# Expert picks in fewer VectorE instructions, two steps per dot, in a one-core decoder layer

## The chip, the cores and the metric

The kernel runs on one core of one Trainium2 chip. The metric is the device time of one execution in microseconds, the median of the runs shown; below it is better.

## What is computed

One layer of a decoder on 256 tokens of width 2048 in float32: a combined projection, three attentions (sliding window with sinks, block-sparse, indexed sparse), gates, an output projection, and then a channel mixer (PEER) with a residual, and a last RMS norm. The change lies in the channel mixer:

```python
def peer_ffn(h, w_q, sub_keys, u_tab, v_tab):
    q = (xt @ w_q).reshape(n, PEER_HEADS, 2, PEER_QDIM // 2)
    s = jnp.einsum("nhpd,hpkd->nhpk", q, sub_keys)           # 8 heads, 2 x 128 scores
    s1, i1 = lax.top_k(s[:, :, 0], PEER_TOPK)                # 16 of 128
    s2, i2 = lax.top_k(s[:, :, 1], PEER_TOPK)
    cand_s = (s1[..., :, None] + s2[..., None, :]).reshape(n, PEER_HEADS, 256)
    cand_i = (i1[..., :, None] * PEER_KEYS + i2[..., None, :]).reshape(n, PEER_HEADS, 256)
    top_s, pos = lax.top_k(cand_s, PEER_TOPK)                # 16 of 256
    experts = jnp.take_along_axis(cand_i, pos, axis=-1)
    g = jax.nn.softmax(top_s, axis=-1)
    a = jax.nn.gelu(jnp.einsum("td,thkd->thk", xc, u_tab[ec]))
    return jnp.einsum("thk,thkd->td", gc * a, v_tab[ec])
```

Each token and head picks 16 of 16384 experts. The expert's row of `u_tab` (2048 floats, 8 KB) is multiplied with the token's hidden vector, the sum goes through a gelu, is weighted with the softmax of the scores, and multiplies the expert's row of `v_tab`.

## The kernel before

The program has one hand-written instruction stream per engine, joined by semaphores. It goes through the weight matrices first: TensorE multiplies, ScalarE and VectorE split every float32 block into a high and a low part (lines 550 and 905). This takes some 740 us. At the end, from about 1590 us on, `v_tab` is streamed as dense blocks and multiplied with a matrix of coefficients (line 1486). Between the two lies the expert stage, which the change touches.

**Units.** The 256 tokens are two tiles of 128 (one token per partition), and there are 8 heads, so 16 units; unit c is tile c // 8 and head c % 8. For a unit, the picks (`pick_step`, lines 1075 to 1131) find the 16 expert numbers, GpSimd gathers 16 times 128 rows of `u_tab` (1 MB each), and VectorE makes 16 dots (`dot`, line 1133), one for each gather: the 2048 products of row and hidden vector, summed per partition, 128 tokens at a time.

**GpSimd.** `phase` (lines 524 to 531) waits until the unit's indices are there (`idx_ok`), copies them to `stage_u` (line 526), and issues the 16 gathers (line 530). The landing place is `u_ring`, four slots of 1 MB. Gather k waits until dot k-4 is done (`dot_ok`), so at most four gathers are ahead of the dots. All instructions are in order: gather 0 of the next unit comes after gather 15 of this one and the copy.

**VectorE.** `phase` (lines 1167 to 1177) runs the 16 dots of unit c, and behind dot k it does step k of the picks of unit c+1. A pick has 13 steps (`PICK_STEPS`): 0 to 3 find 16 of 128 scores in both halves (max, max_index, match_replace) and add all pairs to `cand`; 4 to 7 find 16 of the 256 sums; 8 to 10 turn the positions into two key numbers by comparing with a row of 0 to 15, multiplying with the keys found, and summing, and write `key_all` and `idx_all`; 11 and 12 make the softmax from ScalarE's exponentials. Each step begins with a drain, an instruction that lets VectorE finish what is before it. Step 0 waits for the scores' copy (`sw_ok`). Before dot 0, `gelu_argument` (line 1138) forms the cubic argument of the gelu's tanh for the unit before in three small instructions, ScalarE takes the tanh, and behind dot 0 `coefficients` (line 1147) finishes the unit's coefficients. The first pick (unit 0) runs alone, without dots.

**ScalarE.** At the start of the stage it is in the loop over the 16 blocks of the query projection (lines 783 to 803). It moves TensorE's results out (lines 787 and 789), and between blocks it does the exponentials (`exps_of`), the copy of a unit's scores for the picks (`scores_of`) and the tanh (`tanh_of`) of units 0 to 2. These wait for VectorE, and what is behind them waits too. The scores of unit 1 are copied after block 3; those of unit 2 after block 5, and of unit 3 after block 15, the end of the loop. TensorE's next block needs the evacuation of the block before (`qp_ev`). Afterwards a hardware loop over units follows, and from unit 8 on (`phase`, line 840) ScalarE also builds the one-hot matrices of tile 0 (lines 810 to 823).

**SP.** It issues the loads of the query weights during the first units, and of `v_tab`'s first blocks as the last four dots free the ring (line 446).

Of the kernel before, what the change touches and what calls it, by code (L numbers as in the profile page):

```python
# [30 lines left out]
ALU = mybir.AluOpType  # L31
# [75 lines left out]
def build(nc, x, rel_bias, g_mix, w_in, a_sinks, c_lat_gain, c_w_uk, c_w_uv, w_br_a, w_br_b, w_br_c,  # L107
# [86 lines left out]
    tif = at("tif", 202.3125, [P, 2, PTOP])  # L194
# [3 lines left out]
    thlf = at("thlf", 202.6875, [P, 2, PTOP])  # L198
    esel = at("esel", 202.8125, [P, 2, PTOP])
    eidx = at("eidx", 202.9375, [P, PTOP])  # L200
    texp = at("texp", 203, [P, PTOP])
# [4 lines left out]
    tsum = at("tsum", 203.75, [P, 8])  # L206
# [107 lines left out]
    dot_ok = sem("dot_ok")  # L314
    arg_ok = sem("arg_ok")
# [225 lines left out]
    def _(act):  # L541
# [212 lines left out]
        def exps_of(u):  # L754
            act.wait_ge(top_ok, u + 1)
            nc.scalar.activation(texp[:, :], texp[:, :], ACT.Exp, accum_out=tsum[:, 0:1]).then_inc(ex_ok, 1)
# [26 lines left out]
        for w in range(2 * PH):  # L783
# [67 lines left out]
        phase(PH)
        with act.Fori(PH + 1, NU - 2) as c:
            phase(c)
        phase(NU - 2, scoring=False)
        phase(NU - 1, picking=False, scoring=False)
        tanh_of(NU - 1)
# [26 lines left out]
    def _(dve):  # L883
# [190 lines left out]

        def pick_step(u, step):
# [445 lines left out]
```

## Time and profile before

| | us |
|---|---|
| timed runs | 2371.70, 2367.78, 2370.84 (median 2370.84) |
| span of the profiled execution, first to last instruction | 2368.5 |
| VectorE busy in the span | 1492.5 |
| GpSimd busy | 570.1 |
| one dot, custom instruction of line 1135 (256 of them) | 2.284 |
| first dot, last dot (start) | 783.4, 1588.7 |

The profile records one execution; its own device time is not listed beside the span, and the three timed runs lie between 0.7 us below and 3.2 us above the span. A unit of the expert stage can be followed in a timeline from one dot 0 to the next. Times of instructions on GpSimd count from their start to the end of the work on the engine; for a gather that is when it is issued completely, not when its rows have landed. When rows landed can be read where a dot waited for them: it starts then.

### The profile page before, as it was taken

Reading aid. Unit: us, or ns where it says so; the run is one execution under the profiler, and the core shown is the slowest. Engines: PE = TensorE matmul, PEld = TensorE weight load, DVE = VectorE, ACT = ScalarE, POOL = GpSimd, SP = SyncE. Lnnn points to the kernel's source line nnn. Section 1 sums busy time; section 2 is a strip of 40 time slices with the busy share of each in tenths; the row PEclk is TensorE's granted clock in tenths of the full one; section 3 lists DMA queues with packets and bytes.
Section 4 is the critical chain, followed back from the end, with each engine's and each line's share of the span. In section 5 each row is a group of like instructions: output and inputs, shape, how many; then the busy total and the mean of one; then the engine's idle time right before and its main releaser. Section 6 shows DMA issues by size and latency. Waiting matters only on the chain.

```text
span 2368.5 us, 28340 instructions
## 1 busy us (share of the span) xinstructions
PE 1662.7 (70%) x9817; PEld 1478.0 (62%) x9817; DVE 1492.5 (63%) x2175; ACT 850.4 (36%) x1353; POOL 570.1 (24%) x338
## 2 busy tenths in 40 slices
PE   7999999999998980000011111116999999999997
PEld 6999999999987870000011111115888888888886
DVE  5554444445644788999989999879444444444445
ACT  5444444444343100000044344343334444334443
POOL 0000000001600246676666776640000000000000
PEclk9999999999999995555555555559999999999999
DMA  9555566555576999999989899890555556555553
GB/s 305 152 166 164 168 171 171 169 164 159 179 260 202 370 341 339 340 338 343 331 327 343 328 340 338 318 352 25 173 193 195 195 189 242 191 193 195 195 189 112
DMA packets 300663, 560.38 MB, mean 237 GB/s; under 512 B 9452, under 2 KB 238877, under 8 KB 250430
## 3 DMA queue, kind: packets, MB, share of 16 engines
q1 hardware_dynamic: 260926, 282.20, 37.2%
q0 software_dynamic: 39184, 276.84, 31.4%
q8 instruction: 35, 0.57, 0.1%
q10 hardware_dynamic: 496, 0.58, 0.1%
q14 instruction: 22, 0.18, 0.0%
HBM read 555.34 MB, written 8.44 MB: 238 GB/s over the span
## 4 chain that ended last, share of the span: by engine, by line
PE 60%; DVE 21%; DMA 6%; issue 6%; DVEq 3%; POOL 3%; ACT 1%; POOLq 0%; SPq 0%; ACTq 0%
PE ps L1486 30%; PE ps L1231 20%; DVE u_ring L1135 14%; DMA u_ring<-in_peer_u,stage_u 6%; PE ps L1391 4%; PE ps L1413 3%; DVEq L1081 2%; POOL u_ring L530 1%; DVE ones L1162 1%; POOL stage_u L526 1%; PE ps L1336 1%; PE ps L1317 1%; PE ps L1326 0%; DVE esel L1121 0%; POOL msum L517 0%
## 5 line engine op out<-in xcount | busy, mean ns | idle before, releaser
L1135 DVE CUSTOM_DVE_ANT_0 u_ring<-u_ring,h 128x2048 f32<-128x2048 f32 x256 | 583.9, 2284 | 56.8 <-DMA u_ring<-in_peer_u,stage_u 56.3
L530 POOL DMA_INDIRECT u_ring<-in_peer_u,stage_u x256 | 471.8, 1843 | 306.1 <-DVE dots L1135 247.9
L905 DVE TENSOR_TENSOR w_lo<-raw,w_hi 128x2048 fp32r<-128x2048 f32 x112 | 259.1, 2314 | 332.2 <-ACT w_hi L550 332.0
L1231 PE MATMUL ps<-act_hi,w_hi 128*128 128x256 f32 x1536 | 441.1, 287 | 4.9 <-DVE act_lo L1030 2.9
L1231 PE MATMUL ps<-act_hi,w_lo 128*128 128x256 f32 x1536 | 435.3, 283 | 0.0
L1231 PE MATMUL ps<-act_lo,w_hi 128*128 128x256 f32 x1536 | 435.2, 283 | 0.0
L1486 PE MATMUL ps<-v_hi,c_hi 128*128 128x512 f32 x1024 | 400.4, 391 | 4.1 <-DVE v_lo L1204 4.1
L1486 PE MATMUL ps<-v_lo,c_hi 128*128 128x512 f32 x1024 | 400.7, 391 | 0.0
L1486 PE MATMUL ps<-v_hi,c_lo 128*128 128x512 f32 x1024 | 400.5, 391 | 0.0
L871 ACT ACTIVATE v_hi<-u_ring 128x2048 fp32r<-128x2048 f32 x126 | 241.5, 1917 | 417.1 <-PE ps L1486 417.1
L1462 PE MATMUL ps<-ones 128*128 128x128 f32 x512 | 105.0, 369 | 326.8 <-ACT ones L822 310.2
L550 ACT ACTIVATE w_hi<-raw 128x2048 fp32r<-128x2048 f32 x112 | 214.1, 1912 | 264.2 <-PE ps L1231 219.3
L1462 PEld LDWEIGHTS ps<-ones 128*128 128x128 f32 x512 | 89.7, 264 | 342.4 <-issue 232.5
L1231 PEld LDWEIGHTS ps<-act_hi,w_hi 128*128 128x128 f32 x1536 | 295.2, 192 | 6.1 <-issue 4.0
L1231 PEld LDWEIGHTS ps<-act_lo,w_hi 128*128 128x128 f32 x1536 | 295.4, 192 | 0.3 <-issue 0.2
L1231 PEld LDWEIGHTS ps<-act_hi,w_lo 128*128 128x128 f32 x1536 | 295.1, 192 | 0.0
L1204 DVE TENSOR_TENSOR v_lo<-u_ring,v_hi 128x2048 fp32r<-128x2048 f32 x128 | 292.4, 2285 | 0.0
L1202 DVE TENSOR_TENSOR c_lo<-ct,c_hi 128x256 fp32r<-128x256 f32 x128 | 54.5, 425 | 366.0 <-ACT c_hi L872 366.0
L1454 PE MATMUL ps<-ident,key_all 128*128 128x128 f32 x4 | 1.4, 442 | 321.9 <-DVE cw_all L1153 321.9
L1486 PEld LDWEIGHTS ps<-v_hi,c_hi 128*128 128x128 f32 x1024 | 192.8, 188 | 51.2 <-issue 4.3
L1486 PEld LDWEIGHTS ps<-v_lo,c_hi 128*128 128x128 f32 x1024 | 193.0, 188 | 40.9
L1486 PEld LDWEIGHTS ps<-v_hi,c_lo 128*128 128x128 f32 x1024 | 193.1, 189 | 37.6
(204 smaller groups left out, 1588.5 us busy)
## 6 DMA issues: line engine op xcount, KB each, us to landing
u_ring<-in_peer_v SPq DMA_DIRECT2D x128, 1024.0 KB, 4.9
raw<-in_w_in SPq DMA_DIRECT2D x80, 1024.0 KB
raw<-in_w_out SPq DMA_DIRECT2D x16, 1024.0 KB
wq_raw<-in_peer_w_q SPq DMA_DIRECT2D x16, 1024.0 KB, 8.4
raw<-in_w_br_a SPq DMA_DIRECT2D x16, 512.0 KB
bias_by_query<-bias_by_distance POOLq DMA_DIRECT2D x1, 4096.0 KB, 21.0
bias_st<-bias_by_query POOLq DMA_DIRECT2D x16, 256.0 KB, 4.7
raw<-in_w_br_b SPq DMA_DIRECT2D x16, 256.0 KB
```

The lines of the kernel that those rows point to most:

```text
L530: pool.indirect_dma_start(u_ring[:, k % RING], None, u_tab, bass.IndirectOffsetOnAxis(ap=stage_u[:, par, k:k + 1], axis=0)).then_inc(u_in[ ...
L550: nc.scalar.activation(w_hi[:, j % NHL], raw[:, j % NRAW], ACT.Copy).then_inc(hi_done, 1)
L871: nc.scalar.activation(v_hi[:, j % NHL], u_ring[:, j], ACT.Copy)
L905: nc.vector.tensor_tensor(w_lo[:, j % NHL], raw[:, j % NRAW], w_hi[:, j % NHL].bitcast(F32), ALU.subtract).then_inc(lo_done, 1)
L1135: nc.vector.tensor_tensor_reduce(out=u_ring[:, k % RING], in0=u_ring[:, k % RING], in1=h2[:, tile], scale=1.0, scalar=0.0, op0=ALU.mult, o ...
L1202: nc.vector.tensor_tensor(c_lo[:, j % NHL], ct[:, span(RING * i + j, 1)].rearrange("p a t -> p (a t)"), c_hi[:, j % NHL].bitcast(F32), ALU ...
L1204: nc.vector.tensor_tensor(v_lo[:, j % NHL], u_ring[:, j], v_hi[:, j % NHL].bitcast(F32), ALU.subtract).then_inc(vl_ok, 1)
L1231: last = nc.tensor.matmul(out_ap, w_parts[wp][:, slot, k], act_parts[ap][:, k], start=(k == k0 and m == 0), stop=(k == k1 - 1 and m == 2))
L1391: last = nc.tensor.matmul(ps[:, 2 * (c % 2) + t, :], mg_parts[ap][:, T * k + P * t:T * k + P * t + P], w_wide[wp][:, j % NHL, kk], start=( ...
L1413: last = nc.tensor.matmul(ps[:, J + w % 2, cols], wq_raw[:, (w + NWQ // 2) % NWQ, k], h2T[:, k, cols], start=(k == 0), stop=(k == NK - 1))
L1462: last = nc.tensor.matmul(ps[:, 6 + par, PKEYS * m:PKEYS * m + PKEYS], ones[:, 1, par, m], ones[:, 0, par, m], start=True, stop=True)
L1486: last = nc.tensor.matmul(ps[:, 4 * t + c, :], c_parts[cp][:, j % NHL, P * t:P * t + P], v_parts[vp][:, j % NHL, WIDE * c:WIDE * c + WIDE] ...
```

## The change

Four things are changed, all in the expert stage.

1. The picks use fewer instructions. The indices stay uint32 where they were cast to float32 (`tif`, `thlf`, `eidx` are gone); the two comparisons of 256 elements become one of 512, and the two multiplications likewise; the sum is written to `key_all` directly, and the expert number to `idx_all`. The subtraction of the largest score goes to ScalarE, as the bias of the exponential (`ntop`), which also writes to `cw_all` directly. The scaling by the reciprocal of the sum moves from step 12 into `coefficients`, the half of the gelu into the dot's scale.
2. The gelu's argument: ScalarE squares the dots (`tanh_of`), VectorE needs one instruction after it in place of three. It is done behind dot 0, before it was ahead of it, and the coefficients follow behind dot 1, before behind dot 0.
3. Behind dot k come the steps 2k and 2k+1 of the picks, so they are through behind dot 6. In unit 0 (`first`) they begin behind dot 3.
4. ScalarE's two loops over units are unrolled in Python, since the place of the sum (`tsum`) alternates.

```diff
-        def exps_of(u):
+        def exps_of(u, par):
             act.wait_ge(top_ok, u + 1)
-            nc.scalar.activation(texp[:, :], texp[:, :], ACT.Exp, accum_out=tsum[:, 0:1]).then_inc(ex_ok, 1)
+            nc.scalar.activation(ntop[:, :], ts[:, 0:1], ACT.Copy, scale=-1.0).then_inc(nt_ok, 1)
+            act.wait_ge(nt_ok, u + 1)
+            nc.scalar.activation(cw_all[:, span(PTOP * u, PTOP)], ts[:, :], ACT.Exp, bias=ntop[:, 0:1],
+                                 accum_out=tsum[:, par:par + 1]).then_inc(ex_ok, 1)
...
-        def tanh_of(u):
+        def tanh_of(u, par):
+            act.wait_ge(dot_ok, PTOP * u + PTOP)
+            nc.scalar.activation(gel[:, 0], dots[:, par], ACT.Square, scale=2.0 * math.sqrt(0.044715)).then_inc(sqd_ok, 1)
             act.wait_ge(arg_ok, u + 1)
-            nc.scalar.activation(gel[:, 1], gel[:, 0], ACT.Tanh, scale=math.sqrt(2.0 / math.pi)).then_inc(th_ok, 1)
+            nc.scalar.activation(gel[:, 1], gel[:, 0], ACT.Tanh, scale=2.0 * math.sqrt(2.0 / math.pi)).then_inc(th_ok, 1)
...
-        with act.Fori(3, PH) as c:
-            tanh_of(c - 2)
-            exps_of(c)
+        for c in range(3, PH):
+            tanh_of(c - 2, c % 2)
+            exps_of(c, c % 2)
             scores_of(c + 1)
...
             elif step == 3:
                 for s in range(2):
                     nc.vector.max_index(ti[:, s, 8:16], tv[:, s, 8:16], sc_r[:, s])
+                wait(dve, ex_ok, u)
                 nc.vector.tensor_tensor(cand[:, :, :], tv[:, 0].unsqueeze(2).to_broadcast([P, PTOP, PTOP]),
                                         tv[:, 1].unsqueeze(1).to_broadcast([P, PTOP, PTOP]), ALU.add)
             elif step == 4:
                 nc.vector.max(ts[:, 0:8], flat)
-                nc.vector.tensor_copy(tif[:, :, :], ti[:, :, :])
...
             elif step == 7:
-                nc.vector.max_index(tp[:, 8:16], ts[:, 8:16], flat_r)
-                nc.vector.tensor_scalar(texp[:, :], ts[:, :], ts[:, 0:1], None, ALU.subtract).then_inc(top_ok, 1)
+                nc.vector.max_index(tp[:, 8:16], ts[:, 8:16], flat_r).then_inc(top_ok, 1)
             elif step == 8:
                 nc.vector.tensor_scalar(thl[:, 0], tp[:, :], 4, None, ALU.logical_shift_right)
                 nc.vector.tensor_scalar(thl[:, 1], tp[:, :], PTOP - 1, None, ALU.bitwise_and)
-                dve.drain()
-                nc.vector.tensor_copy(thlf[:, :, :], thl[:, :, :])
             elif step == 9:
-                for s in range(2):
-                    nc.vector.tensor_tensor(pick[:, s], thlf[:, s].unsqueeze(2).to_broadcast([P, PTOP, PTOP]),
-                                            iota_f[:, 0:PTOP].unsqueeze(1).to_broadcast([P, PTOP, PTOP]), ALU.is_equal)
-                dve.drain()
-                for s in range(2):
-                    nc.vector.tensor_tensor(pick[:, s], pick[:, s], tif[:, s].unsqueeze(1).to_broadcast([P, PTOP, PTOP]), ALU.mult)
+                nc.vector.tensor_tensor(pick[:, :, :, :], thl[:, :, :].unsqueeze(3).to_broadcast([P, 2, PTOP, PTOP]), iota_pick,
+                                        ALU.is_equal)
             elif step == 10:
-                nc.vector.tensor_reduce(esel[:, :, :], pick[:, :, :, :], AX.X, ALU.add)
-                dve.drain()
-                nc.vector.scalar_tensor_tensor(out=eidx[:, :], in0=esel[:, 0], scalar=float(PKEYS), in1=esel[:, 1], op0=ALU.mult, op1=ALU.add)
-                nc.vector.tensor_copy(key_all[:, :, span(PTOP * u, PTOP)], esel[:, :, :])
-                dve.drain()
-                nc.vector.tensor_copy(idx_all[:, span(PTOP * u, PTOP)], eidx[:, :]).then_inc(idx_ok, 1)
+                nc.vector.tensor_tensor(pick[:, :, :, :], pick[:, :, :, :], ti[:, :, :].unsqueeze(2).to_broadcast([P, 2, PTOP, PTOP]),
+                                        ALU.mult)
             elif step == 11:
-                dve.wait_ge(ex_ok, u + 1)
-                nc.vector.reciprocal(tsum[:, 1:2], tsum[:, 0:1])
+                nc.vector.tensor_reduce(key_all[:, :, span(PTOP * u, PTOP)], pick[:, :, :, :], AX.X, ALU.add)
             elif step == 12:
-                nc.vector.tensor_scalar(cw_all[:, span(PTOP * u, PTOP)], texp[:, :], tsum[:, 1:2], 0.5, ALU.mult, ALU.mult)
+                nc.vector.scalar_tensor_tensor(out=idx_all[:, span(PTOP * u, PTOP)], in0=key_all[:, 0, span(PTOP * u, PTOP)],
+                                               scalar=float(PKEYS), in1=key_all[:, 1, span(PTOP * u, PTOP)],
+                                               op0=ALU.mult, op1=ALU.add).then_inc(idx_ok, 1)
...
         def gelu_argument(u, par):
-            d = dots[:, par]
-            dve.drain()
-            nc.vector.tensor_tensor(gel[:, 0], d, d, ALU.mult)
-            dve.drain()
-            nc.vector.tensor_scalar(gel[:, 0], gel[:, 0], 0.044715, 1.0, ALU.mult, ALU.add)
-            dve.drain()
-            nc.vector.tensor_tensor(gel[:, 0], gel[:, 0], d, ALU.mult).then_inc(arg_ok, 1)
+            dve.wait_ge(sqd_ok, u + 1)
+            nc.vector.scalar_tensor_tensor(out=gel[:, 0], in0=gel[:, 0], scalar=1.0, in1=dots[:, par],
+                                           op0=ALU.add, op1=ALU.mult).then_inc(arg_ok, 1)
 
         def coefficients(u, par):
 
+            dve.wait_ge(ex_ok, u + 1)
+            nc.vector.reciprocal(rsum_u[:, :], tsum[:, par:par + 1])
             dve.wait_ge(th_ok, u + 1)
             nc.vector.scalar_tensor_tensor(out=coef[:, par], in0=gel[:, 1], scalar=1.0, in1=dots[:, par], op0=ALU.add, op1=ALU.mult)
             dve.drain()
             w = cw_all[:, span(PTOP * u, PTOP)]
-            nc.vector.tensor_tensor(w, coef[:, par], w, ALU.mult).then_inc(cw_ok, 1)
+            nc.vector.scalar_tensor_tensor(out=w, in0=w, scalar=rsum_u[:, 0:1], in1=coef[:, par],
+                                           op0=ALU.mult, op1=ALU.mult).then_inc(cw_ok, 1)
...
             for k in range(PTOP):
+                dot(c, par, tile, k)
                 if k == 0 and not first:
                     gelu_argument(c - 1, 1 - par)
-                dot(c, par, tile, k)
-                if k == 0 and not first:
+                if k == 1 and not first:
                     coefficients(c - 1, 1 - par)
-                if k < PICK_STEPS and top:
-                    pick_step(c + 1, k)
+                step = 2 * (k - 3 if first else k)
+                for n in range(step, step + 2):
+                    if 0 <= n < PICK_STEPS and top:
+                        pick_step(c + 1, n)
```

## Rows read from the trace of the kernel before

**Rows 1.** The page: span, and busy time of each engine.

```profile
span 2368.5 us, 28340 instructions
PE 1662.7 (70%) x9817; PEld 1478.0 (62%) x9817; DVE 1492.5 (63%) x2175; ACT 850.4 (36%) x1353; POOL 570.1 (24%) x338
```

**Rows 2.** The page: the chain that ended last, shares by line.

```profile
PE ps L1486 30%; PE ps L1231 20%; DVE u_ring L1135 14%; DMA u_ring<-in_peer_u,stage_u 6%; PE ps L1391 4%; PE ps L1413 3%; DVEq L1081 2%; POOL u_ring L530 1%; DVE ones L1162 1%; POOL stage_u L526 1%; PE ps L1336 1%; PE ps L1317 1%; PE ps L1326 0%; DVE esel L1121 0%; POOL msum L517 0%
```

**Rows 3.** Windows of the expert stage; the heading line names the columns.

```profile
core 0: us, PE busy (x) PEld busy (x) DVE busy (x) ACT busy (x) POOL busy (x), PEclk, DMA share, GB/s
...
1342.00:1392.00 50.00, 8.29 (x32) 7.12 (x32) 45.36 (x77) 22.34 (x61) 33.52 (x17) 0.50 0.91 336
```

**Rows 4.** Lines 1135 and 530, durations in ns, first and last start.

```profile
L1135 DVE CUSTOM_DVE_ANT_0 u_ring<-u_ring,h x256: 2271/2284/2304, 783.4 to 1588.7; 128x2048 f32<-128x2048 f32 x128
...
  DMA u_ring<-in_peer_u,stage_u: 56.3, 45
...
L530 POOL DMA_INDIRECT u_ring<-in_peer_u,stage_u x256: 935/2127/3030, 775.0 to 1578.2; - x128
```

**Rows 5.** Timeline of unit 8's end and unit 9: start, length, engine, line, operation [idle before].

```profile
1226.33 2.29 DVE L1135 CUSTOM_DVE_ANT_0 u_ring<-u_ring,h 128x2048 f32<-128x2048 f32 x1
...
1228.86 2.29 DVE L1135 CUSTOM_DVE_ANT_0 u_ring<-u_ring,h 128x2048 f32<-128x2048 f32 x1
...
1229.43 2.53 POOL L530 DMA_INDIRECT u_ring<-in_peer_u,stage_u  x1 [2.77 <-DVE dots L1135]
...
1231.51 2.28 DVE L1135 CUSTOM_DVE_ANT_0 u_ring<-u_ring,h 128x2048 f32<-128x2048 f32 x1
1231.97 1.86 POOL L526 COPY stage_u<-idx_all 128x16 uint32 x1
...
1233.72 2.28 DVE L1135 CUSTOM_DVE_ANT_0 u_ring<-u_ring,h 128x2048 f32<-128x2048 f32 x1
1234.72 2.12 POOL L530 DMA_INDIRECT u_ring<-in_peer_u,stage_u  x1 [0.88 <-POOL stage_u L526]
...
1241.42 2.29 DVE L1135 CUSTOM_DVE_ANT_0 u_ring<-u_ring,h 128x2048 f32<-128x2048 f32 x1 [1.85 <-DMA u_ring<-in_peer_u,stage_u]
...
1276.13 2.28 DVE L1135 CUSTOM_DVE_ANT_0 u_ring<-u_ring,h 128x2048 f32<-128x2048 f32 x1
```

**Rows 6.** VectorE's timeline, first pick (no dots); last, a group of 512-element operations.

```profile
764.82 0.49 DVE L1084 MAX8 tv<-sc_w 128x8 f32<-128x128 f32 x2 [11.28 <-ACT sc_w L765]
...
771.52 0.76 DVE L1115 TENSOR_TENSOR pick<-thlf,iota_f 128x256 f32<-128x256 f32 x2
...
774.29 0.17 DVE L1126 CAST idx_all<-eidx 128x16 uint32<-128x16 f32 x1
...
L1160 DVE TENSOR_TENSOR ones<-iota_f,pickT 128x512 f32<-128x512 f32 x32 | 22.1, 692 | 2.6 <-ACT pickT L807 1.8 <-PE ps L1462 0.7
```

**Rows 7.** Timeline: a gather and the dot that waited for it, units 10 and 15.

```profile
1287.28 2.08 POOL L530 DMA_INDIRECT u_ring<-in_peer_u,stage_u  x1 [0.30 <-issue]
...
1295.52 2.29 DVE L1135 CUSTOM_DVE_ANT_0 u_ring<-u_ring,h 128x2048 f32<-128x2048 f32 x1 [0.35 <-DMA u_ring<-in_peer_u,stage_u]
...
1570.54 2.13 POOL L530 DMA_INDIRECT u_ring<-in_peer_u,stage_u  x1 [0.30 <-issue]
...
1577.29 2.29 DVE L1135 CUSTOM_DVE_ANT_0 u_ring<-u_ring,h 128x2048 f32<-128x2048 f32 x1 [0.21 <-DMA u_ring<-in_peer_u,stage_u]
```

**Rows 8.** Timeline of units 0 and 1: VectorE's first step 0, ScalarE's projection loop.

```profile
792.53 0.49 DVE L1084 MAX8 tv<-sc_w 128x8 f32<-128x128 f32 x2 [6.83 <-ACT sc_w L765]
...
822.79 0.38 ACT L787 ACTIVATE qp_st<-ps 128x256 f32<-128x256 f32 x1 [6.53 <-PE ps L1413]
...
830.89 0.38 ACT L787 ACTIVATE qp_st<-ps 128x256 f32<-128x256 f32 x1 [6.53 <-PE ps L1413]
...
841.68 0.22 ACT L770 ACTIVATE gel<-gel 128x16 f32<-128x16 f32 x1 [9.22 <-DVE gel L1145]
...
851.56 0.38 ACT L787 ACTIVATE qp_st<-ps 128x256 f32<-128x256 f32 x1 [8.21 <-PE ps L1413]
...
893.50 0.41 ACT L765 ACTIVATE sc_w<-sc 128x256 f32<-128x256 f32 x1
```

More of the change, by code:

```diff
@@ L193, in build @@
     ti = at("ti", 202.1875, [P, 2, PTOP], U32)
-    tif = at("tif", 202.3125, [P, 2, PTOP])
     ts = at("ts", 202.4375, [P, PTOP])
@@ L197, in build @@
     thl = at("thl", 202.5625, [P, 2, PTOP], U32)
[L198 to L201, printed above, removed]
     dots = at("dots", 203.0625, [P, 2, PTOP])
@@ L205, in build @@
     stage_u = at("stage_u", 203.4375, [P, 2, PTOP], U32)
-    tsum = at("tsum", 203.75, [P, 8])
+    tsum = at("tsum", 203.75, [P, 2])
+    ntop = at("ntop", 203.8125, [P, 1])
+    rsum_u = at("rsum_u", 203.84375, [P, 1])
     one_col = at("one_col", 203.875, [P, 1])
@@ L314, in build @@
     dot_ok = sem("dot_ok")
+    nt_ok = sem("nt_ok")
+    sqd_ok = sem("sqd_ok")
     arg_ok = sem("arg_ok")
@@ L793, in _ @@
             if w == 1:
-                exps_of(0)
+                exps_of(0, 0)
             if w == 3:
@@ L797, in _ @@
             if w == 5:
-                exps_of(1)
+                exps_of(1, 1)
                 scores_of(2)
             if w == 8:
-                tanh_of(0)
+                tanh_of(0, 0)
             if w == 12:
-                exps_of(2)
+                exps_of(2, 0)
         def picks_turned(tile):
@@ L830, in _, with phase @@
         scores_of(3)
-        with act.Fori(3, PH) as c:
-            tanh_of(c - 2)
-            exps_of(c)
+        for c in range(3, PH):
+            tanh_of(c - 2, c % 2)
+            exps_of(c, c % 2)
             scores_of(c + 1)
-        tanh_of(PH - 2)
-        exps_of(PH)
+        tanh_of(PH - 2, 0)
+        exps_of(PH, 0)
         scores_of(PH + 1)
         act.wait_ge(x1_out, 16)
-        def phase(c, picking=True, scoring=True):
-            tanh_of(c - 1)
+        def phase(c, par, picking=True, scoring=True):
+            tanh_of(c - 1, 1 - par)
             if isinstance(c, int) and c == PH:
@@ L847, in phase @@
                 if q == 1 and picking:
-                    exps_of(c + 1)
+                    exps_of(c + 1, 1 - par)
                 if q == 1 and scoring:
                     scores_of(c + 2)
[L851 to L856, printed above, removed]
+        phase(PH, 0)
+        for c in range(PH + 1, NU - 2):
+            phase(c, c % 2)
+        phase(NU - 2, 0, scoring=False)
+        phase(NU - 1, 1, picking=False, scoring=False)
+        tanh_of(NU - 1, 1)
         picks_turned(1)
@@ L1073, in _ @@
         nc.vector.memset(one_col[:, :], 1.0)
+        iota_pick = iota_f[:, 0:PTOP].unsqueeze(1).unsqueeze(1).to_broadcast([P, 2, PTOP, PTOP])
         def pick_step(u, step):
@@ L1133, in dot @@
         def dot(u, par, tile, k):
             dve.wait_ge(u_in[k % RING], 16 * (PTOP // RING) * u + 16 * (k // RING + 1))
-            nc.vector.tensor_tensor_reduce(out=u_ring[:, k % RING], in0=u_ring[:, k % RING], in1=h2[:, tile], scale=1.0, scalar=0.0,
+            nc.vector.tensor_tensor_reduce(out=u_ring[:, k % RING], in0=u_ring[:, k % RING], in1=h2[:, tile], scale=0.5, scalar=0.0,
                                            op0=ALU.mult, op1=ALU.add, accum_out=dots[:, par, k:k + 1]).then_inc(dot_ok, 1)
```

## The prediction

> **What bounds the kernel now.** I read the page first, for the stage that the change touches. VectorE is busy for 63% of the span and TensorE for 70% [rows 1], but these are means over different stages, so the chain of waits comes next: its shares name the dot of line 1135 (14%), the wait for the gathered rows (6%), and GpSimd's lines 530 and 526 (1% each) [rows 2]. All of them lie in the expert stage, where the chain has no TensorE work to speak of. The windows view of one stretch inside that stage shows who is full: in 50 us VectorE works 45.36, GpSimd 33.52, and the 16 DMA engines are busy 0.91 of the time at 336 GB/s; TensorE works 8.29 [rows 3]. Nobody is full all the time: the stage is a loop of three parties. The dots run from 783.4 to 1588.7 us, 255 steps, so 50.5 us for a unit of 16. VectorE waits for rows 56.3 us in all, in 45 places [rows 4]: mostly VectorE sets the pace, and at three or so places of each unit it runs into the ring of four.
>
> The timeline of one unit shows where. Two facts carry the forecast. **First, a GpSimd instruction that starts while a dot runs does not end before it.** The gather issued at 1229.43, inside the dot of 1228.86, takes 2.53 us and ends 0.9 us after the dot; the copy of indices issued at 1231.97 inside the dot of 1231.51 takes 1.86 us; alone, a gather takes 0.94 (the minimum in rows 4 is 935 ns) [rows 4, 5]. **Second, the unit's end has a fixed latency.** Gather 15 waits for dot 11 (start 1226.33, so end 1228.6) and is issued 0.8 us later; then come the copy, 0.88 us of gap, gather 0 of the next unit at 1234.72 for 2.12 us, and its rows land in time for the dot at 1241.42, 4.6 us after the gather's own end, while VectorE sat idle 1.85 us [rows 5]. From the start of dot 11 to the next unit's dot 0 that is 15.1 us. From dot 0 to dot 11 VectorE is the bound: 1241.42 to 1276.13, 34.7 us [rows 5]. Together 49.8, the unit. Dots alone follow each other every 2.21 us (1231.51 to 1233.72) [rows 5], so 11 of them are 24.3 and the small work among them 10.4.
>
> **The change, part by part.** *VectorE's small work.* The first pick runs without dots between: 764.82 to 774.46 [rows 6], 9.6 us for steps 0 to 10. Steps 11 and 12, the argument of the gelu (three instructions and drains) and the coefficients add some 2.4, 12.0 per unit. Of the new sequence: the casts, the subtraction and the key copy go, with their drains, some 0.9 us; the two pairs of 256-element operations (760 ns a pair) become two of 512 elements, for which I take the 692 ns of line 1160, so 0.14 less with their starts [rows 6]. That leaves 8.7 for all 13 steps. The gelu argument becomes one instruction (0.25), the coefficients keep two and gain the reciprocal (0.75). Sum 9.7, which is 2.3 less than before. But the last two steps and the gelu argument lay in the 15.1 us window, under the 1.85 us of waiting, so before dot 11 only 10.4 is replaced by 9.7: a gain of 0.7 us, if nothing else changes.
>
> *The order.* Now all 9.7 lie in the slots of dots 0 to 6, and dots 7 onwards follow without a gap. Dots 7, 8, 9 find their rows landed. Counting from dot 0: seven dots and the 9.7 put dot 7 at 25.2, dots 8 and 9 at 27.4 and 29.6. Gather 10 needs dot 6's end (22.7 + 2.3) plus 0.8, so it is issued at 25.8, inside dot 7. By the first fact it ends at 27.4 + 0.9 = 28.3, and its rows land 4.6 later, at 32.9. VectorE is free at 31.8: it waits 1.1. Gather 11 ends 2.2 later behind dot 8, at 30.5. If its rows take 4.6 again, or 2.5 behind the landing before, dot 11 waits 0.3 more. If a gather so close to the one before pays more, the wait is longer: at a spacing of 2.43 us (0.30 + 2.13) the rows came 4.6 after the gather (1572.67 to 1577.29), at 2.38 (0.30 + 2.08) they came 6.2 after it (1289.36 to 1295.52) [rows 7]. The spacing here, 2.2, is nearer to the second row; that row may have been an accident, so I take the middle, 0.7, and keep 0.3 and 1.1 as bounds. Dot 11 then starts at 24.3 + 9.7 + 1.1 + 0.7 = 35.8 (35.4 to 36.2), where before it was 34.7. The window behind it: gather 15 now also ends behind a dot, the copy behind the next, gather 0 behind dot 14, which by the same counting gives 15.3 in place of 15.1. The new unit is 51.1 us (50.7 to 51.5) against 49.8: **1.3 longer, though VectorE has 2.3 less to do**. From unit 2's to unit 15's dot 0 there are 13 such units: +17 (12 to 22).
>
> *The rule against this change.* The rows show GpSimd held for the length of a dot [rows 5]. The Trainium skill (SBUF — State Buffer, section on the two separate sides) says the pair of ports is locked exclusively for a whole instruction, by a VectorE operation with two SBUF inputs against a GpSimd operation that reads SBUF; the trace agrees, with 2.53 in place of 0.94. The box of the same section names only two-port perf modes as what starves descriptors, and by that the dots would hold nothing; it is the third rival below.
>
> *The first unit.* VectorE stands idle 6.83 us after dot 0, until the scores of the second unit are copied at 792.5 [rows 8]. With step 0 behind dot 3, dots 1 to 3 fill this time; dot 4 can come about 7 us sooner, and the start of unit 1 with it. But not all is kept. ScalarE's projection loop runs beside it: its tanh at 841.68 had waited 9.22 us for unit 0, and the next evacuation, 8.1 us apart before (822.79 and 830.89), would come at 839.0 undisturbed; the loop's end, the scores copied at 893.50, is what VectorE needs for the first pick step of unit 2 [rows 8]. That end moves forward by 841.8 - 839.0 = 2.8, and by up to 1.7 more if the evacuation after it (851.56), which waited 8.21 in place of 6.53, does so no longer. So unit 2 gains 4 (2.7 to 4.5), and 3 of the 7 become a new wait in its slot 0.
>
> *Without a price.* ScalarE now squares the dots, and unrolls its loops. Per unit it adds one activation for the square and one for the negated maximum, about 0.2 each; the square is done while dot 0 runs (2.3 us), the tanh while steps 0 and 1 and dot 1 run. The new wait in step 3 is on the exponentials of the unit before, done long ago, and nothing waits behind it. If the square needed a table load of its own, the cover is still over 1.3; only behind the last dot nothing covers it. There the old chain has three VectorE instructions, the new one a square and one, equal within 0.3; a table load each way would add at most 2.6. POOL and SP issue the same DMAs in the same order. Everything behind the last dot moves with it.
>
> **The sum.** +17 - 4 = +13 us. The span of the profiled execution is 2368.5 [rows 1]; the timed runs are 2367.8 to 2371.7, so it is an ordinary one, some 2 us below the median with what lies around it. Against the median 2370.84: **2384**, own range 12 - 4.5 to 22 - 2.7: 2378 to 2390.
>
> **The rivals.**
> - *The ring holds (faster).* Gather 10's rows are in time for dot 10: it needs to land 1.1 us sooner than counted. Place: the gap-free dots 7 to 9. Then dot 11 starts at 34.0, the window is 15.1, the unit 49.1: 13 x -0.7 - 4 = -13, 2358. For it: VectorE is the busiest engine, 45.4 of 50 [rows 3]. Against it: in unit 15, the dot of 1577.29, with no picks before it, waits 0.21 behind one of 2.29, so 2.5 us from start to start [rows 7].
> - *A mixed price (same).* Only dot 10 waits and half as long, or the picks save 0.7 more than counted: unit 49.8 to 50.3, which with the -4 is 2367 to 2374.
> - *GpSimd is not held at all (faster).* Then every gather takes 0.94, the window is covered, and the unit is VectorE's own 16 x 2.205 + 9.7 = 45.0: 13 x -4.8 - 4, about 2305. The rows with 2.53 and 1.86 [rows 5] speak against it.
> - *The change does not shorten the picks (slower still).* The 512-element operations read uint32 beside float32; no such row is in the trace. Bounds: 692 ns as float32, or twice that. Two such would add 1.4 per unit, before dot 6, so in full: 13 x 1.4 = 18 more, 2402.
>
> **How the numbers follow.** Forecast 0.70; mixed 0.11; ring holds 0.10; not held 0.02; longer picks 0.07. A difference of 0.2% is 4.7 us, what a measurement can tell here. Slower is the forecast with the longer picks: 0.77; faster 0.13 (the two rivals and little else); same 0.10. The forecast's own range is 2378 to 2390; to hold 8 in 10 it reaches down into the mixed case and a little above, 2371 to 2393.
>
> **What would show it.** In the trace after: a unit of 50.7 to 51.5 us; dots 0 to 6 apart by 2.5 to 4.5 us, dots 7 to 9 by 2.2; waits on the gather before dots 10, 11 and 0; more than the 56.3 us that VectorE waits for rows now, nearer 90; gathers 10 to 14 taking over 2 us. Unit 0 without the 6.8 us hole and a wait for the scores in unit 2. VectorE's busy time lower by some 30 us in the stage. Wrong would be: dots 10 and 11 with no wait (first rival), gathers of 0.94 behind gap-free dots (third), or pick operations over 1 us (fourth).

## The result

The changed kernel takes **2385.9 us** (median of nine, 2375.5 to 2391.2), the kernel before, in nine runs beside it, 2371.0 (2364.3 to 2373.1). The ratio is 1.0061, with a 95% interval of 1.0047 to 1.0076: slower by 0.6%, though VectorE has less to do. The profiled execution of the changed kernel took 2387.9, with a span of 2386.6, so the spans differ by 18.1 and the medians by 14.9.

In the new file line 1135 (the dot) has become 1131, 530 (the gather) 529 and 526 (the copy) 525. The page of the changed kernel: span and busy times, which answer to [rows 1], the chain's shares, which answer to [rows 2], and the groups of the dot and of the gather (busy us, mean ns of one | idle before them and what ended it).

```profile
span 2386.6 us, 27746 instructions
...
PE 1660.7 (70%) x9817; PEld 1477.4 (62%) x9817; DVE 1474.1 (62%) x2015; ACT 857.3 (36%) x1385; POOL 506.6 (21%) x338
...
PE ps L1483 29%; PE ps L1228 20%; DMA u_ring<-in_peer_u,stage_u 7%; DVEq L1087 5%; PE ps L1410 4%; DVE u_ring L1131 4%; POOL u_ring L529 4%; PE ps L1388 4%; DVE ones L1157 1%; PE ps L1333 1%; PE ps L1314 1%; POOL stage_u L525 1%; PE ps L1414 0%; PE ps L1323 0%; POOL msum L516 0%
...
L1131 DVE CUSTOM_DVE_ANT_0 u_ring<-u_ring,h 128x2048 f32<-128x2048 f32 x256 | 583.6, 2289 | 111.8 <-DMA u_ring<-in_peer_u,stage_u 109.1
L529 POOL DMA_INDIRECT u_ring<-in_peer_u,stage_u x256 | 419.6, 1639 | 389.1 <-DVE dots L1131 337.6
```

VectorE's busy time fell by 18.4 us, and the span rose by 18.1. In the chain the dot falls from 14% to 4%, and the gather on GpSimd rises from 1% to 4%, the wait for rows from 6% to 7%. What rose is VectorE's wait for rows, from 56.3 [rows 4] to 109.1. GpSimd works less than before (506.6 against 570.1) and the median gather is shorter; the trace of line 529 says so, with the count of the dot's waits beside it:

```profile
L1131 DVE CUSTOM_DVE_ANT_0 u_ring<-u_ring,h x256: 2270/2290/2395, 784.2 to 1608.3; 128x2048 f32<-128x2048 f32 x128
...
  DMA u_ring<-in_peer_u,stage_u: 109.1, 102
...
L529 POOL DMA_INDIRECT u_ring<-in_peer_u,stage_u x256: 932/1115/3055, 775.2 to 1597.9; - x128
```

The median gather took 2127 ns [rows 4] and now takes 1115. That median falls by more than the holding does, since it lies between two groups: 121 of the 256 gathers take over 1.8 us, where it was 141. What changed is which ones are held. The timeline of unit 8 shows it (start, length, engine, line, operation [idle before]; the beginning of the unit, one gather of its middle, and its end up to dot 0 of unit 9):

```profile
1196.06 2.29 DVE L1131 CUSTOM_DVE_ANT_0 u_ring<-u_ring,h 128x2048 f32<-128x2048 f32 x1 [0.56 <-DMA u_ring<-in_peer_u,stage_u]
...
1211.40 0.94 POOL L529 DMA_INDIRECT u_ring<-in_peer_u,stage_u  x1 [2.75 <-DVE dots L1131]
1211.60 2.27 DVE L1131 CUSTOM_DVE_ANT_0 u_ring<-u_ring,h 128x2048 f32<-128x2048 f32 x1
...
1221.34 2.28 DVE L1131 CUSTOM_DVE_ANT_0 u_ring<-u_ring,h 128x2048 f32<-128x2048 f32 x1
...
1221.86 2.58 POOL L529 DMA_INDIRECT u_ring<-in_peer_u,stage_u  x1 [2.91 <-DVE dots L1131]
...
1223.55 2.29 DVE L1131 CUSTOM_DVE_ANT_0 u_ring<-u_ring,h 128x2048 f32<-128x2048 f32 x1
...
1224.74 1.91 POOL L529 DMA_INDIRECT u_ring<-in_peer_u,stage_u  x1 [0.30 <-issue]
...
1225.76 2.29 DVE L1131 CUSTOM_DVE_ANT_0 u_ring<-u_ring,h 128x2048 f32<-128x2048 f32 x1
...
1228.96 2.29 DVE L1131 CUSTOM_DVE_ANT_0 u_ring<-u_ring,h 128x2048 f32<-128x2048 f32 x1 [0.90 <-DMA u_ring<-in_peer_u,stage_u]
...
1232.05 2.29 DVE L1131 CUSTOM_DVE_ANT_0 u_ring<-u_ring,h 128x2048 f32<-128x2048 f32 x1 [0.79 <-DMA u_ring<-in_peer_u,stage_u]
...
1235.36 2.29 DVE L1131 CUSTOM_DVE_ANT_0 u_ring<-u_ring,h 128x2048 f32<-128x2048 f32 x1 [1.01 <-DMA u_ring<-in_peer_u,stage_u]
...
1238.17 2.29 DVE L1131 CUSTOM_DVE_ANT_0 u_ring<-u_ring,h 128x2048 f32<-128x2048 f32 x1 [0.51 <-DMA u_ring<-in_peer_u,stage_u]
...
1238.47 2.05 POOL L525 COPY stage_u<-idx_all 128x16 uint32 x1
...
1240.59 2.29 DVE L1131 CUSTOM_DVE_ANT_0 u_ring<-u_ring,h 128x2048 f32<-128x2048 f32 x1
...
1241.40 2.33 POOL L529 DMA_INDIRECT u_ring<-in_peer_u,stage_u  x1 [0.88 <-POOL stage_u L525]
...
1248.32 2.29 DVE L1131 CUSTOM_DVE_ANT_0 u_ring<-u_ring,h 128x2048 f32<-128x2048 f32 x1 [2.85 <-DMA u_ring<-in_peer_u,stage_u]
```

The dots of 1221.34, 1223.55 and 1225.76 (7, 8 and 9) follow without a gap. Gather 10 is issued 0.5 us into dot 7, takes 2.58 and ends 0.8 after that dot; gather 11 ends in the same way behind dot 8, at 1226.65. Dot 10 then waits until 1228.96, dot 11 until 1232.05, and dots 12 and 13 wait for their rows too. From its dot 0 to the next one unit 8 takes 52.3 us, where it took 50.4 before (1190.99 to 1241.42). Over the stage, dot 0 of unit 2 is at 886.37 and dot 0 of unit 15 at 1561.38: 675.0 us for 13 units, 51.9 each. Before it was 891.55 to 1543.02, 651.5 in all or 50.1 each.

The first units, in the timeline: dot 3 of unit 0 and the first pick step, dot 0 of unit 2, and ScalarE beside it.

```profile
791.87 2.29 DVE L1131 CUSTOM_DVE_ANT_0 u_ring<-u_ring,h 128x2048 f32<-128x2048 f32 x1 [0.34 <-DMA u_ring<-in_peer_u,stage_u]
...
794.25 0.49 DVE L1090 MAX8 tv<-sc_w 128x8 f32<-128x128 f32 x2
...
886.37 2.29 DVE L1131 CUSTOM_DVE_ANT_0 u_ring<-u_ring,h 128x2048 f32<-128x2048 f32 x1 [2.56 <-DMA u_ring<-in_peer_u,stage_u]
...
889.90 0.42 ACT L767 ACTIVATE sc_w<-sc 128x256 f32<-128x256 f32 x1
890.22 0.20 ACT L772 ACTIVATE gel<-dots 128x16 f32<-128x16 f32 x1
890.45 0.18 DVE L1136 SCALAR_TENSOR_TENSOR gel<-gel,dots 128x16 f32<-128x16 f32 x1 [1.79 <-ACT gel L772]
```

The idle 6.83 us before the first step 0 [rows 8] is gone: the step starts at 794.25 with no wait, behind dot 3 (791.87). Unit 1 begins at 834.8 in place of 841.6, unit 2 5.2 us sooner; and a new wait stands behind unit 2's dot 0, 1.79 us, for ScalarE.

Last, the group of the two new 512-element operations in a stretch from 1050 us on:

```profile
L1120 DVE TENSOR_TENSOR pick<-pick,ti 128x512 f32<-128x512 f32 x10 | 6.9, 693 | 0.9
L1117 DVE TENSOR_TENSOR pick<-thl,iota_f 128x512 f32<-128x512 uint32 x10 | 6.9, 692 | 0.7
```

### The profile page after: what moved, and what is told of

Its sections match the earlier page's. It is cut to its first block, busy times and chain, and to the rows that moved or that the text cites. A ratio compares the mean times of both kernels' runs of the same rounds, so it can differ in the third digit from the quotient of the medians.

```text
span 2386.6 us, 27746 instructions
## 1 busy us (share of the span) xinstructions
PE 1660.7 (70%) x9817; PEld 1477.4 (62%) x9817; DVE 1474.1 (62%) x2015; ACT 857.3 (36%) x1385; POOL 506.6 (21%) x338
## 4 chain that ended last, share of the span: by engine, by line
PE 61%; DVE 11%; DMA 8%; issue 8%; DVEq 6%; POOL 5%; ACT 1%; POOLq 0%; SPq 0%; ACTq 0%
PE ps L1483 29%; PE ps L1228 20%; DMA u_ring<-in_peer_u,stage_u 7%; DVEq L1087 5%; PE ps L1410 4%; DVE u_ring L1131 4%; POOL u_ring L529 4%; PE ps L1388 4%; DVE ones L1157 1%; PE ps L1333 1%; PE ps L1314 1%; POOL stage_u L525 1%; PE ps L1414 0%; PE ps L1323 0%; POOL msum L516 0%
## 5 line engine op out<-in xcount | busy, mean ns | idle before, releaser
L1131 DVE CUSTOM_DVE_ANT_0 u_ring<-u_ring,h 128x2048 f32<-128x2048 f32 x256 | 583.6, 2289 | 111.8 <-DMA u_ring<-in_peer_u,stage_u 109.1
L529 POOL DMA_INDIRECT u_ring<-in_peer_u,stage_u x256 | 419.6, 1639 | 389.1 <-DVE dots L1131 337.6
```

Of the source, the lines that this page charges most:

```text
L529: pool.indirect_dma_start(u_ring[:, k % RING], None, u_tab, bass.IndirectOffsetOnAxis(ap=stage_u[:, par, k:k + 1], axis=0)).then_inc(u_in[ ...
L1131: nc.vector.tensor_tensor_reduce(out=u_ring[:, k % RING], in0=u_ring[:, k % RING], in1=h2[:, tile], scale=0.5, scalar=0.0, op0=ALU.mult, o ...
```

## The experiments

The theory: the picks really are shorter and the first unit really is faster; the two steps per dot lose more than both, because they leave the last nine dots of a unit without anything between them (bare dots, below). It has two halves that can be told apart: GpSimd is held while such dots run, and the ring of four asks for rows faster than they land. All ratios are against the kernel before; where no ratio is given, the run is a single one.

### One step per dot, in the changed kernel

```diff
-                step = 2 * (k - 3 if first else k)
-                for n in range(step, step + 2):
+                step = 2 * (k - 3) if first else k
+                for n in range(step, step + (2 if first else 1)):
```

> The changed kernel, but from unit 1 on one step per dot again (steps 0 to 12 behind dots 0 to 12); unit 0 as in the change. Theory (the picks are shorter, the bunching is what costs: gap-free dots 7 to 9 hold GpSimd's gathers, so dots 10 to 15 wait for rows): a unit of 48.3 us in place of some 51.9, so 13 x -1.5 against the kernel before and some -5 from the first unit: about 2346 us, ratio 0.990. Rival A (the new pick instructions themselves cost more, by length or by what they block): the unit stays above 49.8, ratio 1.00 or more. Rival B (the new place of the gelu argument and the coefficients costs): likewise no faster than before.

Measured: 2350.65 us (2344.0 to 2365.2, four runs; before 2370.47), ratio 0.9914 (0.9892 to 0.9936). The one line turned +15 us into -20. Two steps per dot therefore cost 35 us in this kernel. The profiled execution is the slowest of the four (2365.2, the others 2344.0 to 2351.3), and its trace shows little of the gain. Its waits for rows are 90.3 us. Its unit is 48.4 us as a sum of the median distances from dot to dot in units 3 to 14, as expected, but 50.2 in the mean of units 2 to 14 (882.11 to 1534.61), since five of them take 51.5 to 52.6; why those are late was not found. So the 20 us rest on the times of the four runs, and not on this trace.

### Two steps per dot, in the kernel before

```diff
-                if k < PICK_STEPS and top:
-                    pick_step(c + 1, k)
+                for n in range(2 * k, 2 * k + 2):
+                    if n < PICK_STEPS and top:
+                        pick_step(c + 1, n)
```

> The kernel before, with two steps per dot and nothing else changed (unit 0 too, from dot 0). Theory (bunching costs by itself): the unit goes from 49.8 to about 53.1 us, the total to 2371 + 14 x 3.2 = 2416 us. Rival A (the new instructions are what costs, bunching is free): the unit stays at 49.8, the total at 2371.

Measured in one run: 2420.3, 50 us above 2370.47; the unit is 53.35 us (898.7 to 1592.3 for 13 of them). The timeline shows a dot with no gap before it, and, two dots on, the first that waits:

```profile
1247.84 2.29 DVE L1135 CUSTOM_DVE_ANT_0 u_ring<-u_ring,h 128x2048 f32<-128x2048 f32 x1
...
1253.17 2.29 DVE L1135 CUSTOM_DVE_ANT_0 u_ring<-u_ring,h 128x2048 f32<-128x2048 f32 x1 [0.82 <-DMA u_ring<-in_peer_u,stage_u]
```

The two dots behind that one wait 0.85 and 0.98 as well. The loss needs none of the new instructions. From here to the changed kernel it is -34: that is what the new instructions and the first unit are worth when the order is bad, and 12 of it lie ahead of dot 0 of unit 2 (898.7 against 886.4).

### Only the first unit, in the kernel before

```diff
-                if k < PICK_STEPS and top:
-                    pick_step(c + 1, k)
+                step = 2 * (k - 3) if first else k
+                for n in range(step, step + (2 if first else 1)):
+                    if 0 <= n < PICK_STEPS and top:
+                        pick_step(c + 1, n)
```

> The kernel before, with only unit 0 changed: its steps go two per dot, from the fourth dot on. Theory (the idle time behind dot 0 is filled, but ScalarE's projection loop takes some back at unit 2): unit 1 starts 6 to 7 us earlier, unit 2's slot 0 waits for the scores, unit 3 starts 3 to 5 us earlier, and the total is 2371 - 4 = 2367 us, ratio 0.998. Rival: nothing is taken back and all 7 us arrive, 2364; or the projection loop or the shared DMA takes it all, 2371.

Measured: 2364.58 (ten runs), ratio 0.9980 (0.9967 to 0.9993), so 4.7 us gained (1.7 to 7.8). Dot 0 comes 9.1 us sooner in unit 1 (832.5), and in unit 2 at 882.3. Of these 9.1, 3.3 were there already in this execution when the stage began (first dot at 780.07, before 783.4); unit 0 itself is 5.8 shorter (52.4 against 58.2). Unit 2 then takes 51.5 and gives back over 1 of it in a wait for ScalarE's tanh:

```profile
886.23 0.17 DVE L1150 SCALAR_TENSOR_TENSOR coef<-gel,dots 128x16 f32<-128x16 f32 x1 [1.59 <-ACT gel L770]
```

### Two steps per dot from the fourth dot on, in every unit

```diff
-                step = 2 * (k - 3 if first else k)
+                step = 2 * (k - 3)
```

> The changed kernel, but in every unit the steps, still two per dot, begin behind dot 3 and are through behind dot 9. Theory (what counts is where the dots without work between them lie, not how many steps go behind one): dots 0 to 2 have no picks between them but their gathers and those of 4 to 6 are early enough in the unit's first burst, and the gathers for dots 10 to 15 start in the gaps of dots 6 to 9, so the unit falls to about 48.0 us and the total to some 2343 us, ratio 0.988. Rival (two steps behind one dot cost in any place): a unit of 51 to 52 us, ratio 1.005.

Measured: 2363.66 (ten runs), ratio 0.9979 (0.9965 to 0.9993). The sign is right, the size missed: 7 us gained where 28 were expected. (The profiled execution is the longest of the ten.) The trace of unit 8 shows where the rest went. Dots 0 to 2 now have no pick step behind them, and fewer bare dots are left at the end, yet GpSimd's queue is behind at the start too:

```profile
1192.16 2.29 DVE L1131 CUSTOM_DVE_ANT_0 u_ring<-u_ring,h 128x2048 f32<-128x2048 f32 x1
1192.82 2.44 POOL L529 DMA_INDIRECT u_ring<-in_peer_u,stage_u  x1 [2.79 <-DVE dots L1131]
...
1194.95 2.28 DVE L1131 CUSTOM_DVE_ANT_0 u_ring<-u_ring,h 128x2048 f32<-128x2048 f32 x1
1195.57 2.48 POOL L529 DMA_INDIRECT u_ring<-in_peer_u,stage_u  x1 [0.30 <-issue]
...
1198.35 2.18 POOL L529 DMA_INDIRECT u_ring<-in_peer_u,stage_u  x1 [0.30 <-issue]
...
1202.76 2.29 DVE L1131 CUSTOM_DVE_ANT_0 u_ring<-u_ring,h 128x2048 f32<-128x2048 f32 x1 [1.25 <-DMA u_ring<-in_peer_u,stage_u]
```

Three gathers in a row are held for over 2 us, and dot 4 (1202.76) waits for its rows although there were two pick steps between it and dot 3. I had counted only the bare dots at the end of a unit.

### The dots of the second tile read the hidden vector from PSUM

VectorE's dot has two inputs in SBUF. PSUM is the other memory on the core, in which TensorE leaves its results. In this run the one that stays the same for 128 dots is copied once to PSUM by ScalarE (four banks that are free from there on); GpSimd's work is untouched.

```diff
+        act.wait_ge(s2_ev, 2 * PH)
+        nc.scalar.activation(ps[:, 0:4, :], h2[:, 1].rearrange("p (a b) -> p a b", b=512), ACT.Copy).then_inc(hp_ok, 1)
...
-            nc.vector.tensor_tensor_reduce(out=u_ring[:, k % RING], in0=u_ring[:, k % RING], in1=h2[:, tile], ...
+            h = ps[:, 0:4, :].rearrange("p a b -> p (a b)") if tile else h2[:, 0]
+            nc.vector.tensor_tensor_reduce(out=u_ring[:, k % RING], in0=h, in1=u_ring[:, k % RING], ...
```

> The changed kernel, but for tile 1 (units 8 to 15) the dots read the hidden vectors from PSUM (copied there once by ScalarE), so they have one input in SBUF; units 0 to 7 are as they were. Theory (a dot with two SBUF inputs holds GpSimd until it ends, and that makes the gathers late): in units 8 to 14 every gather takes about 0.94 us, whatever VectorE does, and the unit falls from some 52 to 47 us; units 2 to 7 stay at 51 to 52. Total some 33 us below the changed kernel, 2353. Rival (the ring of four and the DMA engines' 2.5 us per gather limit the dots without picks, the hold of GpSimd is hidden behind them): units 8 to 14 stay within 1 us of units 2 to 7, total 2384 to 2390.

Measured in one run: 2356.8, before 2367.6. Inside this execution units 2 to 7 take 51.9 us (883.9 to 1195.1) and units 8 to 14 48.4 (1195.1 to 1533.8). Gathers and index copies, by tile, in a stretch of either kind (min/median/max ns):

```profile
L530 POOL DMA_INDIRECT u_ring<-in_peer_u,stage_u x76: 932/1905/2897, 899.1 to 1138.7; - x76
L526 POOL COPY stage_u<-idx_all x5: 1799/1986/2052, 929.0 to 1132.5; 128x16 uint32 x5
...
L530 POOL DMA_INDIRECT u_ring<-in_peer_u,stage_u x109: 936/936/1123, 1202.3 to 1528.6; - x109
L526 POOL COPY stage_u<-idx_all x7: 201/202/203, 1233.3 to 1522.7; 128x16 uint32 x7
```

and the two kinds of dot, on the same kernel's page:

```profile
L1135 DVE CUSTOM_DVE_ANT_0 u_ring<-h,u_ring 128x2048 f32<-128x2048 f32 x128 | 291.7, 2288 | 52.1 <-DMA u_ring<-in_peer_u,stage_u 50.9
L1135 DVE CUSTOM_DVE_ANT_0 u_ring<-ps,u_ring 128x2048 f32<-128x2048 f32 x128 | 290.6, 2286 | 30.2 <-DMA u_ring<-in_peer_u,stage_u 28.2
```

With one operand out of SBUF the dot is as long as before, and no gather of that stretch is held: the hold comes from where VectorE's operands lie. The edit also swaps the order of the two operands, but it does so in both tiles, and in the first the hold is still there. The hold is worth 3.5 us per unit by these two means. That is between 2.8, if unit 2 is left out (55.0 us, with a wait for ScalarE in it), and 3.8 against the same units 8 to 14 of the changed kernel (52.2).

### Both tiles from PSUM, two steps per dot

The edit of the run before for both tiles; the steps stay as in the changed kernel.

> The changed kernel as it is (two steps per dot), but the dots of both tiles read the hidden vectors from PSUM. Theory (bunching costs mainly through the hold of GpSimd): without the hold, a unit of two steps per dot is within some 2 us of one with one step per dot (46.4 us in the sixth experiment): 48.4 us, as tile 1 had in the fifth, against 3 us between the two orders with the hold. Total 2331 + 13 x 2 = 2357 less the share of the long wait in unit 2, which a slower unit 1 makes shorter: 2350 to 2357. Rival (the order costs by the ring alone): the difference between the two orders stays at 3 us or more per unit, total 2370 or more.

Measured in one run: 2339.4, before 2369.4; the unit is 48.4 (938.8 to 1519.6 for 12), as in the half of the run before. That is better than I expected by 11 us, and far from the rival's 2370. Against the changed kernel's 2385.9 it is 46 us, and 48.5 between the two spans. Units 3 to 14, 3.6 each, give 43 of these 48.5; units 0, 1 and the last one give 12 more, the stage begins 1.5 later, and unit 2 loses 5, as VectorE waits 8.9 us in it for ScalarE's square. In the kernel before, each of the 142 gathers that start inside a dot ends after it, by 0.81 to 0.85 us; here 136 of 137 end before it.

### Both tiles from PSUM, one step per dot

> One step per dot from unit 1 on, as in the first experiment, and the dots of both tiles read the hidden vectors from PSUM. Theory (short picks, spread out, and no hold): VectorE alone sets the pace, 16 dots of 2.2 us and 9.7 us of small work, so a unit of about 45.6 us, and the total is 2371 - 13 x 4.2 - 7, about 2309 us, ratio 0.974. Rival (the hold is hidden): no faster than the first experiment, 2346. Should a dot that reads PSUM take longer than 2.28 us, each 0.05 us costs 13.

Measured: 2330.54 (four runs), ratio 0.9842 (0.9826 to 0.9859), 21 us worse than expected. The units are 46.7 us (948.2 to 1508.7 for 12), 1.1 more than I had put, some 13 in all. More lies in unit 2, which takes 67.6; the first units, 11 us shorter where I had put 7, give part of it back. The timeline of unit 2:

```profile
892.12 9.11 PE L1418 MATMUL ps<-h2T,wq_raw 128*128 128x256 f32 x32 [6.91 <-DMA wq_raw<-in_peer_w_q]
...
902.73 0.41 ACT L768 ACTIVATE sc_w<-sc 128x256 f32<-128x256 f32 x1
904.83 0.20 ACT L773 ACTIVATE gel<-dots 128x16 f32<-128x16 f32 x1
905.07 0.18 DVE L1142 SCALAR_TENSOR_TENSOR gel<-gel,dots 128x16 f32<-128x16 f32 x1 [22.10 <-ACT gel L773]
```

VectorE waits 22.1 us behind dot 0 of unit 2 (that dot started at 880.67) for ScalarE's square, which stands behind the end of the projection loop, whose last block waited 6.9 us for its weights. The gathers come sooner now, and their transfers lie beside that of the weights; that they delay it is the likely reason, and was not tried alone.

The windows from 1000 to 1500 us of four kernels: before, changed, both tiles from PSUM with two steps, and with one (columns as in [rows 3]):

```profile
1000.00:1500.00 500.00, 52.37 (x203) 44.98 (x203) 452.67 (x770) 142.72 (x390) 327.68 (x170) 0.50 0.91 334
```

```profile
1000.00:1500.00 500.00, 50.63 (x195) 43.24 (x195) 427.14 (x638) 141.44 (x395) 266.85 (x163) 0.50 0.88 322
```

```profile
1000.00:1500.00 500.00, 56.82 (x219) 48.56 (x219) 454.92 (x690) 159.94 (x448) 158.37 (x174) 0.50 0.93 344
```

```profile
1000.00:1500.00 500.00, 56.86 (x219) 48.60 (x219) 468.13 (x724) 162.93 (x452) 163.28 (x181) 0.50 0.96 359
```

The DMA share, the last column but one, orders these kernels as their units do (50.1, 51.9, 48.4, 46.7). So do the GB/s and the busy times of every engine but GpSimd: a shorter unit puts more of the same work into 500 us, so the column shows that the DMA engines are nearly full (0.96) in the fastest, and doesn't show a cause. With the hold gone there is still 1.7 us per unit between two steps and one. My reading, for which no run stands alone, is this: bare dots use up a slot every 2.2 us, while in the changed kernel the slots of dots 0 to 5, with the picks, last 3.3 to 4.4 (medians), and there the ring is full: the rows of dots 4 to 7 lie landed for 4.0 to 4.8 us before their dot, where it was 1.1 to 1.9 before the change. What the DMA engines could have moved in that time is missing at the end of the unit.

### The best version

Both tiles from PSUM and one step per dot; in unit 2 the picks come two per dot behind dot 8, so that they don't wait for the end of the projection loop, and ScalarE takes unit 1's tanh inside that loop, after block 14.

```diff
+            if w == 14:
+                tanh_of(1, 1)
...
+                from_dot = 3 if first else late
+                step = 2 * (k - from_dot) if from_dot else k
+                for n in range(step, step + (2 if from_dot else 1)):
...
+        phase(2, 0, 0, late=8)
```

> The sixth experiment (one step per dot, hidden vectors in PSUM), and in unit 2 the picks, two steps per dot, begin behind dot 8 alone, with ScalarE's square and tanh of unit 1 moved ahead of the projection loop's last block. In the sixth experiment VectorE stood 22.1 us in unit 2, since that square came behind the projection loop, which had waited for its last weights (6.9 us and more). Theory: most of that time is filled, the wait falls to under 5 us, the total is 2331 - 17 = 2314 us, ratio 0.977. Rival (the weights come as much later as the gathers come sooner, or the picks that are moved late delay unit 3's gathers): 2325 to 2331.

Measured: 2314.06 (five runs, 2309.6 to 2317.5; before 2369.4), ratio 0.9767 (0.9751 to 0.9784): as expected, and faster than both kernels. Unit 2 takes 53.1 us, the others 46.5. The wait for ScalarE is gone; the price is in dot 0 of unit 3, whose indices are late:

```profile
901.34 0.49 DVE L1098 MAX8 tv<-sc_w 128x8 f32<-128x128 f32 x2
...
930.28 2.29 DVE L1140 CUSTOM_DVE_ANT_0 u_ring<-ps,u_ring 128x2048 f32<-128x2048 f32 x1 [4.72 <-DMA u_ring<-in_peer_u,stage_u]
...
L530 POOL DMA_INDIRECT u_ring<-in_peer_u,stage_u x256 | 242.7, 948 | 473.8 <-DVE dots L1140 453.7
```

## Why the prediction was right

The median, 2385.9, lies 1.9 above the 2384 given, inside the forecast's own range, and the mechanism is the forecast's: bare dots hold the late gathers, and dots 10 and 11 wait. That it came so near is in part luck, for the two profiled executions differ by 18.1, where the sum said 13. Point by point:

- **The sum.** Predicted +17 for 13 units and -4 for the first units. In the profiled executions it is +23.5 (675.0 - 651.5) and -5.2. The rest cancels: the last unit's dots take 1.3 more, and from the last dot to the end it is 779.8 before and 778.3 after. So the term of the units was mis-sized: +1.8 per unit in place of 1.3, just over my upper bound of 1.7 (51.5 - 49.8). My 49.8 for the old unit, put together from two neighbouring ones, was 0.3 short as well: the mean is 50.1. Part of this is the execution: its span is 18.1 above the one before, the medians differ by 14.9.
- **Dot 0 to dot 11.** Predicted 35.8 with 0.7 for the disputed wait of dot 11, bounds 35.4 and 36.2. Unit 8 has 36.0, the mean of units 3 to 14 is 36.2. Gather 11 ended at 1226.65 and its rows were there 5.4 us later, for dot 12 it was 6.5. So the row at a spacing of 2.38 [rows 7] was no accident, as I had allowed it might be. Dot 11's own wait is 0.79 in unit 8 and 0.95 in the mean, between the 0.7 taken and the upper bound of 1.1; dot 10 waits 0.90 and 1.00, where I had 1.1. Why rows take longer when gathers are 2.2 us apart is not settled; the dots from 10 to 13, which all waited, started 3.1, 3.3 and 2.8 us apart, and that is how far apart the rows came.
- **Dot 11 to the next dot 0.** Predicted 15.3; unit 8 has 16.3 (1232.05 to 1248.32), and 15.6 is the median. I counted dots 12 to 14 as landed in time, and they weren't: 8.5 us pass from dot 11 to dot 14 in place of 6.6. After dot 14 it went as counted: gather 0 ends at 1243.73, 0.85 us after the dot (1240.59 and 2.29), and the rows come 4.6 later.
- **The hold.** Gather 10 took 2.58 and gather 0 2.33, and both ended 0.8 to 0.9 us after a dot, as the first fact says. The copy took 2.05 and also outlasted its dot (1238.17 and 2.29), but by less than 0.1. The run with one operand in PSUM shows the cause: 936 ns for a gather, 202 for a copy. The Trainium skill (SBUF — State Buffer, section on the two separate sides) gives VectorE and GpSimd one pair of ports, locked for a whole instruction by a VectorE operation with two SBUF inputs against a GpSimd one that reads SBUF; the run agrees. It also says that whichever comes second fully blocks; here a gather that started 0.2 us before a dot (1211.40 and 1211.60) took its 0.94 and the dot 2.27, so neither was blocked, and the measurement decides. The same holds for all dots of the kernel before: none took over 2304 ns [rows 4].
- **The third rival (no hold)** was wrong as a forecast, and wrong in its price too: I gave it 2305, with a unit of 45.0 that is VectorE's alone. The run that removes the hold from the changed kernel gives a unit of 48.4 and 2339. Something else stands next, the landing of rows in the bare stretch: VectorE still waits 2.6 us per unit for rows there. The price of that rival had no such term.
- **The picks.** The 512-element operations take 692 and 693 ns, as taken, so the fourth rival falls. The small work between dot 0 and dot 7 of unit 8 is 9.8 us (1196.06 to 1221.34, less seven dots), where I had 9.7. VectorE's busy time fell by 18.4, not by some 30, so 1.15 per unit: the rest of the 2.3 us per unit was drains and starts, which are not busy time. The gain is real: by its four runs the kernel with one step per dot is 20 us faster than the one before, of which the first unit accounts for some 5.
- **The first unit.** Predicted: unit 1 about 7 us sooner, unit 2 4 (2.7 to 4.5); measured 6.8 and 5.2, the second a little over its bound. The new wait in unit 2 is there, at 1.79 us in place of 3, and it is ended by ScalarE's square, not by the copy of the scores just ahead of it. I had priced the square at nothing, with dot 0 as cover, but it too stands behind the projection loop. Here the two come 0.3 us apart and it cost little; with both tiles from PSUM the same place cost 8.9 us with two steps per dot and 22.1 with one.
- **Waits for rows** came to 109.1, where I said nearer 90. I had counted dots 10, 11 and 0; dots 12 to 15 wait 2.5 us per unit besides (mean of units 3 to 14), half of it at dot 15, which waited 0.7 before.

The lesson of my misses in the experiments is the same one twice. I costed an edit in the stretch that I was looking at (the end of a unit, or the steady units), and the loss came up where the edit made something else early: the start of the unit where all picks began at the fourth dot, the projection's last block where GpSimd was no longer held.

## What to carry to other kernels

Where a consumer works from a short ring, small work between its steps is not only cost: it is what spaces the requests. Packing it together frees time in one place and makes a burst elsewhere, so compare the shortest distance of two steps with the distance at which the producer can deliver, not the averages. If GpSimd instructions next to a VectorE operation have two lengths, look for the VectorE operation that reads two SBUF operands, and try one of them in PSUM before shortening anything.

## What was unexpected of the hardware

- A 128x2048 float32 dot with one operand in PSUM takes 2286 ns, with both in SBUF 2288; GpSimd beside it goes from a median of 1905 to 936 ns for a gather, and from 1986 to 202 for a copy of 128x16.
- The hold is one-sided: a dot that starts inside a gather is not longer (2.27 us). A gather that starts inside a dot ends 0.81 to 0.85 us after it, 142 times of 142 in the kernel before.
- With gathers of 1 MB issued 2.2 us apart, rows land 5.4 and 6.5 us after the gather's end, where it was 4.5 and 4.6 with more than 5 us between their ends (gathers 10 and 0); with the hold gone and one step per dot, the DMA engines are busy 0.96 of the time at 359 GB/s.
